# Causal attention in steps of four key tiles, with the causal mask added by VectorE, in an eight-core decoder layer

## What is computed

```python
qa = concatenate([q_nope, q_rope])          # per head 128 + 64
ka = concatenate([k_nope, k_rope (shared)])
s = einsum('bhqd,bshd->bhqs', qa, ka) / sqrt(192)
s = where(k_pos <= q_pos, s, -inf)          # causal
ha = softmax(s) @ v * silu(a_z)
```

```python
h = rms_norm(x); proj = h @ w_in            # all projections
merged = g_m * (hm @ w_br_m) + g_a * (ha @ w_br_a) + g_c * (hc @ w_br_c)
out = rms_norm(x + merged @ w_out)
```

## Time and profile before

| | us |
|---|---|
| median of 3 runs (2750.35 to 2952.0) | 2751.95 |
| the profiled execution, its own time | 2748.97 |
| span of its slowest core, core 1 | 2747.7 |
| spans of the eight cores | 2732.5 to 2747.7 |
| TensorE busy on core 1 | 2693.6 (98%) |
| VectorE, ScalarE, GpSimd busy | 1059.3, 892.9, 617.0 |
| matmuls, of them masks | 14037, 128 |

### The profile page before, as it was taken

The page is one execution under the profiler, slowest core; times in us unless marked ns, Lnnn a source line. Parts: engine busy times, 40 slices in busy tenths (PEclk is TensorE's granted clock), DMA queues, the critical chain, the costliest instruction groups (busy, mean ns, idle before and its releaser), DMA issues.

```text
span 2747.7 us, 41837 instructions; the slowest of 8 cores (2732.5 to 2747.7 us)
## 1 busy us (share of the span) xinstructions
PE 2693.6 (98%) x14037; PEld 1300.4 (47%) x14037; DVE 1059.3 (39%) x1788; ACT 892.9 (32%) x1741; POOL 617.0 (22%) x924
## 2 busy tenths in 40 slices
PE   7999899999999999999999999999999999999998
PEld 3544344564446644454555444444444444444444
DVE  6645377548576556244434311111111111111433
ACT  5532356436565454254544211111111111110212
POOL 0003100100210121277760122222222222221000
PEclk9999999999999999999999999999999999999999
DMA  9657724532544324556645744445475544447562
GB/s 252 130 131 159 193 62 108 117 98 55 105 104 108 78 41 86 96 141 155 166 107 147 170 77 76 78 74 79 77 165 92 95 75 77 76 78 131 193 206 87
DMA packets 142211, 312.38 MB, mean 114 GB/s; under 512 B 14833, under 2 KB 73009, under 8 KB 134961
## 3 DMA queue, kind: packets, MB, share of 16 engines
q0 software_dynamic: 42048, 134.27, 30.6%
q1 hardware_dynamic: 95634, 162.32, 18.9%
q10 hardware_dynamic: 4320, 13.11, 1.5%
HBM read 371.22 MB, written 72.68 MB: 162 GB/s over the span
## 4 chain that ended last, share of the span: by engine, by line
PE 92%; DMA 5%; ACT 1%; DVE 1%; issue 1%; POOL 1%; SPq 0%; ACTq 0%; POOLq 0%; DVEq 0%
PE bk L290 91%; DMA xt<-x 1%; DMA xo<-x 1%; DMA QRT<-ob 1%; DMA cz<-CZ 0%; DMA HMT<-hm 0%; PE bk L514 0%; SPq L135 0%; DMA QNT<-ob 0%; DMA mb<-BH 0%; PE bk L535 0%; PE bk L1188 0%; PE bk L1234 0%; DVE ro L303 0%; PE bk L1338 0%
## 5 line engine op out<-in xcount | busy, mean ns | idle before, releaser
L290 PE MATMUL bk<-hT,wg 128*128 128x512 bf16 x3072 | 682.3, 380 | 0.0
L290 PE MATMUL bk<-w,hT 128*128 128x512 bf16 (+1 forms) x3072 | 598.3, 345 | 7.5 <-DMA w<-wA 2.9
L290 PE MATMUL bk<-hT,w 128*128 128x512 bf16 x2112 | 489.6, 380 | 0.0
L290 PEld LDWEIGHTS bk<-hT,wg 128*128 128x128 bf16 x3072 | 300.5, 98 | 361.5 <-issue 1.6
L290 PEld LDWEIGHTS bk<-w,hT 128*128 128x128 bf16 x3072 | 296.3, 98 | 251.8 <-issue 16.2
L294 ACT ACTIVATE sh<-bk 128x512 f32<-128x512 f32 x184 | 109.8, 597 | 850.1 <-PE bk L290 850.1
L290 PE MATMUL bk<-hb,wb 128*128 128x512 bf16 x1536 | 346.7, 379 | 0.0
L290 PEld LDWEIGHTS bk<-hT,w 128*128 128x128 bf16 x2112 | 204.9, 98 | 228.8 <-issue 4.7
L310 DVE SCALAR_TENSOR_TENSOR tm<-sh,bk 128x512 f32<-128x512 f32 x124 | 85.3, 688 | 559.2 <-PE bk L290 559.2
L290 PEld LDWEIGHTS bk<-hb,wb 128*128 128x128 bf16 x1536 | 150.1, 98 | 181.1
L303 DVE TENSOR_TENSOR den<-den,Pa 128x512 f32<-128x512 f32 (+3 forms) x288 | 186.4, 647 | 103.4 <-ACT Pa L294 75.1
(11 more groups left out here) (180 smaller groups left out, 2433.1 us busy)
## 6 DMA issues: line engine op xcount, KB each, us to landing
wg<-wGB POOLq DMA_DIRECT2D x96, 512.0 KB, 5.3
w<-wA POOLq DMA_DIRECT2D x48, 516.0 KB, 9.2
wb<-wGB POOLq DMA_DIRECT2D x96, 256.0 KB, 4.1
xt<-x SPq DMA_DIRECT2D x16, 1024.0 KB, 13.3
xo<-x SPq DMA_DIRECT2D x16, 1024.0 KB, 6.8
out<-xo SPq DMA_DIRECT2D x15, 1024.0 KB, 7.4
wo<-wOUT POOLq DMA_DIRECT2D x4, 2048.0 KB, 17.5
w<-wA POOLq DMA_DIRECT2D x16, 500.0 KB, 12.2
```

Of the source, the lines that this page charges most:

```text
L290: fw.op("pe", lambda e: e.matmul(bk[o] if not isinstance(o, bass.AP) else o, lhsT=lhsT, rhs=rhs, start=start, stop=stop), reads=reads, wri ...
```

## The change

Attention: `emit_S` now takes four key tiles at once: four matmuls with `kn`, four with `kr`, then for the last four tiles VectorE adds `mneg` to 128 columns of each bank in place (no mask matmuls), four exponentials, four sums. The scores of the next group of four are written before the products of the present group, and across blocks and heads too. There are eight tiles `Pa` and three `den`; `f3` stands at the same tick as `f2`.

```diff
-                    def emit_S(kt):
-                        for j in range(2):
-                            k = kt + j
...
-                        if kt >= 4 * qb:
-                            for k, n, qc, kc_, (bs, r_bs) in prs:
-                                mm(bs, r_bs, (slice(None), slice(0, 128)), identb[:], mneg[:], False, True, [RC, mneg.r])
...
+            groups = [(h, qb, kq) for h in range(8) for qb in range(4) for kq in range(qb + 1)]
+            def emit_S(h, qb, kq):
...
+                for k in range(4 * kq, 4 * kq + 4):
+                    n = (4 * qb + 4 - max(k, 4 * qb)) * 128
+                    its.append((k, n, slice(4 * qb * 128 + 512 - n, 4 * qb * 128 + 512), slice(k * 128, (k + 1) * 128), SBk.next()))
+                for k, n, qc, kc_, (bs, r_bs) in its:
+                    mm(bs, r_bs, (slice(None), slice(0, n)), kn[:, kc_], qn[:, qc], True, False, [kn.r, qn.r])
+                for k, n, qc, kc_, (bs, r_bs) in its:
+                    hf = slice(64 * (k % 2), 64 * (k % 2) + 64)
+                    mm(bs, r_bs, (slice(None), slice(0, n)), kr[hf, kc_], qr[hf, qc], False, True, [kr.r, qr.r])
+                if kq == qb:
+                    for k, n, qc, kc_, (bs, r_bs) in its:
+                        tt("dve", bs[:, 0:128], bs[:, 0:128], mneg[:], ALU.add, [mneg.r], [r_bs])
...
+            nxt = emit_S(*groups[0])
+            yield 7 * MM
+            for gi, (h, qb, kq) in enumerate(groups):
+                cur_ = nxt
+                if gi + 1 < len(groups):
+                    nxt = emit_S(*groups[gi + 1])
+                    yield 6 * MM
...
+                for k, p, n in cur_:
+                    mm(po, r_po, (slice(None), slice(512 - n, 512)), vx[:, k, :], p[:, 0:n], k == 0, k == 4 * qb + 3, [vx.r, p.r])
                     tick()
+                    yield MM * n / 512
-                later(5, f3)
+                later(4, f3)
```

```diff
-            ob = Ring(tiles("ob", 6, [128, S], BF16))
+            ob = Ring(tiles("ob", 6, [128, S], BF16, n=2))
-            marks.add("MLA0")
-                    for ci in (2, 0, 1):
+                    for ci in ((2, 0, 1) if pr or tb else (0, 1, 2)):
+                    if tb % 2:
+                        c = slice(tb * 512 - 512, tb * 512 + 512)
...
+                            fw.dma("sp", QNT_d[hh * 128:(hh + 1) * 128, c], o3[ci][:, c], reads=[o3[ci].rs[tb // 2]], accs=[dr("QNT", hh)])
-                    if t_ == 3:
+                    if t_ == 1:
                         marks.add("ML")
-                loads_g(c + 2)
-                    fw.dma("sp", HMT_d[cp // 4, :, cp % 4, :], hm2[0][:].rearrange("p a b -> p (a b)"), reads=[hm2[0].r], accs=[dr("HMT", cp // 4)])
+                    fw.dma("act", HMT_d[cp // 4, :, cp % 4, :], hm2[0][:].rearrange("p a b -> p (a b)"), reads=[hm2[0].r], accs=[dr("HMT", cp // 4)])
-            yield 4.0
+            yield 8.0
             P["mtail"]()
...
-            yield 4.0
+            yield 1.0
-            for _ in range(4):
-                bload()
...
+                bload()
-            wo_load(3, mem.alloc("wo3", [128, 16, 512], BF16))
...
+            wo_load(3, wo3)
-        sides = [(mla_gen, "MLA0", 0.38), (mlstm_gen, "ML", 0.34), (c_gen, "CZ0", 0.7)]
+        sides = [(mla_gen, "MLA", 0.345), (mlstm_gen, "V1", 0.34), (c_gen, "CZ0", 0.7)]
```

More of the change, by code:

```diff
@@ L687, in p1_gen, with part, half @@
             cqnT, ckvnT = P["cqnT"], P["ckvnT"]
-            ob = Ring(tiles("ob", 6, [128, S], BF16))
-            def part(o, c, bk, r_bk, first):
-                evac_copy(o[:, c], bk[:, 0:512], [r_bk], [o.r] if first else [], [] if first else [o.r])
+            ob = Ring(tiles("ob", 6, [128, S], BF16, n=2))
+            def part(o, tb, bk, r_bk):
+                evac_copy(o[:, tb * 512:(tb + 1) * 512], bk[:, 0:512], [r_bk], *half(o, tb))
+            def half(o, tb):
+                return ([], [o.rs[tb // 2]]) if tb % 2 else ([o.rs[tb // 2]], [])
             def rotate(o, tb, bk, r_bk):
@@ L698, in rotate @@
                 tt("dve", t2[64:128, :], bk[0:64, 0:512], sinT[0:64, cols], ALU.mult, [r_bk, sinT.rs[tb]], [], [t2.r])
-                tt("pool", o[:, cols], t1[:], t2[:], ALU.add, [t1.r, t2.r], [o.r] if tb == 0 else [], [o.r] if tb else [])
+                tt("pool", o[:, cols], t1[:], t2[:], ALU.add, [t1.r, t2.r], *half(o, tb))
             def part_v(o, u, bk, r_bk):
@@ L755, in ev @@
                             else:
-                                copy("act", o[:, cols], bk[:, 0:512], [r_bk], [o.r] if tb == 0 else [], [o.r] if tb else [])
+                                copy("act", o[:, cols], bk[:, 0:512], [r_bk], *half(o, tb))
                         yield from fm_unit(wb, ci * 128, 128, lambda kc: cqnT[:, kc, cols], [cqnT.rs[tb]], ev, q=4)
[L758 to L763, removed]
+                    if tb % 2:
+                        c = slice(tb * 512 - 512, tb * 512 + 512)
+                        for ci in range(2):
+                            hh = 2 * pr + ci
+                            fw.dma("sp", QNT_d[hh * 128:(hh + 1) * 128, c], o3[ci][:, c], reads=[o3[ci].rs[tb // 2]], accs=[dr("QNT", hh)])
+                        fw.dma("sp", QRT_d[pr * 128:(pr + 1) * 128, c], o3[2][:, c], reads=[o3[2].rs[tb // 2]], accs=[dr("QRT", pr)])
             paced["on"] = True
@@ L886, in v_block @@
             if jv == 1:
+                marks.add("V1")
                 mem.release(bif)
@@ new lines, in emit_S @@
+                for k, n, qc, kc_, (bs, r_bs) in its:
[4 more added lines that the diff above has]
+                        tt("dve", bs[:, 0:128], bs[:, 0:128], mneg[:], ALU.add, [mneg.r], [r_bs])
+                res = []
+                for k, n, qc, kc_, (bs, r_bs) in its:
+                    p = Ps.next()
+                    act(p[:, 0:n], bs[:, 0:n], AF.Exp, [r_bs], [p.r], scale=SC)
+                    if k == 0:
+                        copy("dve", acc[:], p[:], [p.r], [acc.r])
+                    else:
+                        o = 512 - n
+                        tt("dve", acc[:, o:512], acc[:, o:512], p[:, 0:n], ALU.add, [acc.r, p.r], [acc.r])
+                    res.append((k, p, n))
```

78 lines of the change are left out of this document (30 added, 48 removed).

## The result

The kernel before takes 2751.23 us as the median of four runs, the changed one 2844.17 us. The ratio is 1.034, with a 95% interval from 1.031 to 1.036: **slower by 3.4%**, 93 us where the prediction had 0.2% less; the two profiled executions lie 94 us apart.

What follows compares the result with a forecast made beforehand. It took TensorE, busy 2693.6 of 2747.7 us, as the bound. Gains of -51.6 and new waits of +46 gave -5.6 us: 2743.4 on the profiled execution, 2746 us as a median, range 2704 to 2772.

Steps and rivals of the forecast that it cites:

- Changes of rows: Attention scores on TensorE: groups of four halve 320 changes between 128 and 64 rows, 0.10 us each: -16.0 us.
- rival (d): Attention scores: the second kr pair's weight loads are exposed by 0.10 us each time: 2754 us, chance 0.08.
- Mask: Attention: 64 pairs of mask matmuls leave TensorE for VectorE adds, nothing waiting soon for the exponentials: -7.7 us.
- rival (b): qk0 to qk2: VectorE's queue becomes the bound and delays ScalarE's evacuations and dense banks: 2780 us, chance 0.12.
- Waits that go: TensorE's waits for late transfers and products (ob, hm, hmt, rdc, Pa, e) vanish, with their clock: -27.9 us together.
- rival (c): Transfer waits return elsewhere, at first scores or in the mLSTM; 25 of 27.9 us stay: 2771 us, chance 0.12.
- Wait 1: Attention: the fourth score matmul after f2 waits for the bank Ln must read, at 16 places: +21 us.
- Wait 2: Blocks v0 and v1: a dense bank waits for GIF behind four sums on VectorE, at 18 places: +19 us.
- Wait 3: qk blocks: masks and sums burst on VectorE's queue, and ScalarE's exponentials wait for masks: +4 us, range 0 to 40.
- Wait 4: Attention's first loads, issued only after uq's last store, land about as their cover ends: +2 us, from 0 to 8.
- Rival (a): New waits at Ln's bank and GIF are covered by slack, 3 us of each staying: 2712 us, chance 0.28.

Runs made afterwards that it cites:

- e8: Changed kernel with first loads within uq, f1 with the last product, key sum in the block's own bank, sums spread one per product: ratio 1.007, 2767 us.
- e12: Kernel before, with pairs kept and only the causal mask moved from TensorE matmuls to VectorE adds: ratio 1.006, runs of 2762 and 2766 us.
- e4: Changed kernel with the causal mask as TensorE matmuls again, still in steps of four: a single run of 2842.6 us.
- e3: Changed kernel with f2 writing the sum over the keys into the block's own bank, not the score ring: ratio 1.021, runs of 2807 to 2810 us.
- e7: Changed kernel with a group's four sums issued one at each product of the group before: ratio 1.034, 2841 us.
- e2: Changed kernel with the attention's first loads issued within uq again, as before the change: ratio 1.028, runs of 2822 to 2830 us.
- e1: Changed kernel with the old attention (pairs, 2.5 per product, TensorE masks, share 0.38), its loads still behind uq: ratio 1.004, runs of 2760 and 2762 us.
- e6: Changed kernel with f1 issued with a block's last product and the sum over the keys in the block's own bank: runs of 2789 and 2791 us.
- e9: As e8, with the causal mask as matmuls on TensorE again: ratio 1.000, 2749 us.
- e10: As e9, with f4 issued two products earlier, at 5 in place of 7: ratio 0.996, 2737 us.
- e5: Changed kernel with f1 issued with a block's last product instead of one product later: ratio 1.032, runs of 2827 and 2844 us.
- e11: As e10, with the first of each group's four sums on GpSimd: ratio 0.994, runs of 2732 to 2734 us.

## Why the prediction was wrong, point by point

It was wrong on the far side: +98 us on its median, outside the range, at a chance that it had put at 0.04. Its gains on TensorE hold; what failed is the list of new waits, which was too short, the price of two entries, and the waits that were to go.

- **Changes of rows, -16.0: right.** Group and gaps in the trace are as computed, the second kr pair is hidden, and rival (d) is false. With it falls, for this kernel, the rule of the Trainium skill (TensorE: Matmul & The Clock Gate, Part 3, "The mechanism") as the prediction applied it: the pair's weights lie on the same rows as those in use and load beside them.
- **Mask, -7.7: right on TensorE (the 128 mask matmuls before took 8.2 us from start to start), wrong as a whole.** "Nothing waits for the exponentials soon" is the sentence that failed. In the kernel before, where the product stands nearer behind its scores, the same edit cost 15 us; in steps of four with the rest repaired it cost 18. The 0.28 us of an add was right; its price is its place in a queue on which another engine's queue waits. In e8 this is the mechanism of rival (b), VectorE's queue in the qk blocks with ScalarE's evacuation behind it; in e12 it is the product that waits, not the evacuation. Rival (b) was drawn for the changed kernel, where TensorE waits for neither y nor pre and taking the adds away changed nothing that one run can tell (e4).
- **Waits that go, -27.9: mis-sized, 8 came.** ob, hm and Pa went (15.2 us), rdc ahead of the cross-attention nearly (2.5 to 0.3). But hmt did not (2.2 and 2.4), and the waits for e, kw and mk grew by 9.1 us together, with the mLSTM's clock at 0.74 over 20 us. On the profiled core some 8 us of waiting went for good and no clock: rival (c) in this part.
- **Wait 1, the fourth score bank, +21: right in kind, 29.9 in size.** Of the 20 cases 10 lie between 1.47 and 1.63 us where 1.55 was computed; two are 4.4 us, where ha holds up the table load, since rba is one tile. Those two alone make 5.7 of the 9 us that were missing. Its removal gave 34 us (e3), because clock goes with it.
- **Wait 2, GIF, +19: right, 17.4 us** and 15 places, and in the group shown to 0.1 us in each step. But it could not be had back alone (e7).
- **Wait 3, VectorE's queue in qk, +4 with a range to 40: the wrong place.** TensorE waited for neither y nor pre; it waited for hi, and for lo behind hi (and in e3, with rba gone, for ua). hia and loa, 26.8 us, appear in no term. The prediction counted how many matmuls stand between f2 and the scores, and not how far f2 stands from f1. Three calls of tick lie between them in both kernels, but a call stood for 2.5 to 3 matmuls' worth of the attention's share and now stands for one: the median room for hi went from 4.31 to 1.49 us. That is the step that failed first: the prediction put the wait for f1's results at nothing.
- **Wait 4, the first loads, +2 with 8 as a bound: 18.2 us.** The chain of waits has the load that came last (issued at, us to landing):

```profile
293.05 20.42 DMA qn<-QNT
```

  It takes 20.4 us to land and not 7.4, at a DMA share of 0.97 to 1.01. The median landing was used for a moment in which all other loads of the attention and of the weights are in flight. e2 gives 17 us for it.
- **Clock: no term for a loss.** 108 us at the lower level against 22. A part of them TensorE would have idled anyway; from the starts of its matmuls, those at the lower level cost 34 us on the profiled core against 8. Eleven stretches at the lower level stand beside waits of the attention, the first loads not counted; not all waits had one (1.24 and 1.63 us at 740 to 743 us stand at the full clock).
- **Rival (a), the cover holds: false** in every part.

The sum by the measured sizes, on the profiled core: -16 - 8 of matmuls; +92 from the five lines; -8 from the other waits; +26 of clock. That is +86, and the span grew by 94; where the remaining 8 us lie is not shown.

What was shown by an edit: the part of the attention as a whole (e1), the first loads (e2), the bank with its clock (e3), f1's place on top of it (e6), the mask (e9, e12) and f4 (e9 to e10). What was only read from the traces: that the spacing of the products took the room from hi, since no run has steps of four at the old spacing of 2.5 (moving f1, e5 and e6, changes its room and its place in VectorE's queue together); that the clock falls because of the clusters of waits, which no run separates from the waits themselves; and why e and kw are late in the mLSTM, where its loads of mb (BH) land late and ScalarE stands at them.

## What to carry to other kernels

When steps are merged on the critical engine, measure in the old trace, for each side chain, the distance from every link to the next in time, and compute it again at the new spacing; the slack was in the spacing, and a merged step takes it from all links at once. The time of an instruction moved to another engine is its place in that engine's queue, and the bill is paid by the queue that waits for it: two adds of 0.29 us on VectorE cost more than the 0.12 us of TensorE that they replaced. And repair all links of one chain before judging any: the mask's return to TensorE gave nothing that one run can tell alone (e4) and 18 us once the chain's other links were mended (e8 to e9).

## What the runs showed of the hardware

- In this trace the lower clock stands at clusters of short waits too, not only at long ones: around waits of 2.37, 0.89 and 1.16 us within 6 us the granted clock is 0.70 over ten. The cost can then be more than the waits' own time. In e3 the waits for rba, hia and loa fell by 48.0 us and those for ua, pre and y rose by 27.6, so 20 us less waiting; the time at the lower level fell from 108 to 73 us (mean clock 0.987), and the kernel was 34 us faster.
- A table load of 1.28 us started only behind what its successor waits for: the bank (1.68 us at 435.83), and in another place a tile in SBUF that another engine still reads (4.10 us for ha).
- Four matmuls on 64 rows behind each other cost one exposure of 0.10 us, as two did; the third's weights load while the first streams, on the same rows (kr in x4, 0.54 us from start to next).
- A load of 512 KB landed in 20.4 us where the median of its kind is 6.6 us in the same execution; kr, qr, kn and vx, the other first loads, and weights were in flight with it, and kn and vx took 19.6 and 21.0 us.
- GpSimd's sum of 512 columns with float output takes 1.21 us against VectorE's 0.69 (e11); 48 of them and 32 copies of 0.63 us beside VectorE's work cost nothing that shows in the time.
